# Steady products read their moving tile from the last token to the first, and write the result bank backwards

## The reference, cut to what matters

```
x <- LN_a(alpha*x + 0.5*SwiGLU_1(x))        w_gu: 1024 x 5632, w_down: 2816 x 1024
h  = x @ W_in                               26 column tiles of 128 (some made up of two pieces)
y  = [NSA | sliding-window attention | HGRN2](h) @ W_out
x <- LN_b(alpha*x + y)
x <- LN_c(alpha*x + 0.5*SwiGLU_2(x))
x <- x + sigmoid(x W_g + b_g) * (p W_p)
```

## Time and profile before

| what | value |
|---|---|
| median of 2 runs | 2225.23 us |
| both runs | 2224.98 and 2225.49 us |
| span of the profiled execution, first to last instruction | 2226.4 us |
| mean granted TensorE clock over the span | 0.998 |
| PE busy, share of the span | 2188.5 us, 98% |
| DVE busy | 1134.1 us, 51% |
| ACT busy | 902.1 us, 41% |
| DMA, mean rate | 91 GB/s |

### The profile page before, as it was taken

How to read it: one execution, slowest core, us unless ns; L and a number is a source line. 1 busy time by engine, 2 the same in 40 slices (tenths; PEclk the granted TensorE clock), 3 DMA queues, 4 the chain that set the end, 5 groups by cost and what they waited for, 6 DMA issues and landing times.

```text
span 2226.4 us, 30811 instructions
## 1 busy us (share of the span) xinstructions
PE 2188.5 (98%) x12675; PEld 1807.6 (81%) x12675; DVE 1134.1 (51%) x1966; ACT 902.1 (41%) x1447; POOL 137.8 (6%) x128
## 2 busy tenths in 40 slices
PE   9999999999999999999999999999999999999999
PEld 7888889877668888888888888898776788888888
DVE  4333345888867333343643333358887663333454
ACT  4223224555656322322632222255466462232234
POOL 0000011210001000012000000112200100000110
PEclk9999999999999999999999999999999999999999
DMA  5333333322222333332333333333322233333322
GB/s 167 97 102 95 88 95 90 99 65 70 81 72 67 104 95 98 106 89 85 107 95 95 100 100 86 98 80 99 77 67 67 67 95 96 101 98 97 95 88 72
DMA packets 384219, 202.76 MB, mean 91 GB/s; under 512 B 17360, under 2 KB 381776, under 8 KB 384080
## 3 DMA queue, kind: packets, MB, share of 16 engines
q1 hardware_dynamic: 383520, 200.15, 31.7%
q10 hardware_dynamic: 560, 0.66, 0.1%
HBM read 198.68 MB, written 2.10 MB: 90 GB/s over the span
## 4 chain that ended last, share of the span: by engine, by line
PE 82%; DVE 9%; ACT 6%; issue 2%; DMA 1%; POOL 0%; SPq 0%; DVEq 0%; ACTq 0%
PE banks L254 24%; PE banks L255 24%; PE banks L256 24%; DVE lev L1241 2%; ACT xhi L353 1%; PE banks L1518 1%; DVE w_lo L246 1%; DVE att L1277 1%; ACT lev L1121 1%; ACT w_hi L240 1%; ACT xT L354 1%; PE banks L1505 1%; PE banks L1459 1%; PE banks L305 1%; PE banks L311 1%
## 5 line engine op out<-in xcount | busy, mean ns | idle before, releaser
L246 DVE TENSOR_TENSOR w_lo<-w_raw,w_hi 128x1024 fp32r<-128x1024 f32 (+2 forms) x370 | 452.5, 1226 | 831.6 <-ACT w_hi L240 831.3
L254 PE MATMUL banks<-xhi,w_hi 128*128 128x512 f32 (+1 forms) x1936 | 758.1, 392 | 1.0 <-DVE w_lo L246 1.0
L256 PE MATMUL banks<-xhi,w_lo 128*128 128x512 f32 (+1 forms) x1936 | 749.7, 387 | 0.0
L255 PE MATMUL banks<-xlo,w_hi 128*128 128x512 f32 (+1 forms) x1936 | 749.7, 387 | 0.0
L240 ACT ACTIVATE w_hi<-w_raw 128x1024 fp32r<-128x1024 f32 (+2 forms) x370 | 376.0, 1018 | 810.0 <-PE banks L256 796.7
L254 PEld LDWEIGHTS banks<-xhi,w_hi 128*128 128x128 f32 x1936 | 365.6, 189 | 75.8 <-issue 1.6
L256 PEld LDWEIGHTS banks<-xhi,w_lo 128*128 128x128 f32 x1936 | 364.1, 188 | 74.6
L255 PEld LDWEIGHTS banks<-xlo,w_hi 128*128 128x128 f32 x1936 | 364.5, 188 | 72.5 <-issue 1.0
L254 PE MATMUL banks<-hhi,w_hi 128*128 128x512 f32 (+1 forms) x792 | 293.4, 371 | 0.0
L256 PE MATMUL banks<-hhi,w_lo 128*128 128x512 f32 (+1 forms) x792 | 289.5, 365 | 0.0
L255 PE MATMUL banks<-hlo,w_hi 128*128 128x512 f32 (+1 forms) x792 | 289.4, 365 | 0.0
(11 more groups left out here) (274 smaller groups left out, 2002.0 us busy)
## 6 DMA issues: line engine op xcount, KB each, us to landing
w_raw<-in_ffn_w_gu_dram SPq DMA_DIRECT2D x176, 512.0 KB, 4.0
w_raw<-in_ffn_w_down_dram SPq DMA_DIRECT2D x64, 512.0 KB, 4.0
w_raw<-in_w_in_dram SPq DMA_DIRECT2D x48, 512.0 KB, 4.1
w_raw<-in_ffn_w_down_dram SPq DMA_DIRECT2D x32, 384.0 KB, 3.5
w_raw<-in_w_out_dram SPq DMA_DIRECT2D x32, 256.0 KB, 2.9
w_raw<-in_ple_gate_w_dram SPq DMA_DIRECT2D x16, 512.0 KB, 3.7
w_raw<-in_cmp_k_w_dram SPq DMA_DIRECT2D x16, 256.0 KB, 2.8
w_raw<-in_cmp_v_w_dram SPq DMA_DIRECT2D x16, 256.0 KB, 3.2
```

The costliest lines, as they stand in the source:

```text
L246: dve.tensor_tensor(part_view(wlo, n), raw_view(split_at[n]).rearrange("p k n -> p (k n)"), part_view(whi, n), ALU.subtract).then_inc(sems ...
L254: pe.matmul(bank, w_hi, x_hi, start=first, stop=False)
L255: pe.matmul(bank, w_hi, x_lo, start=False, stop=False)
L256: return pe.matmul(bank, w_lo, x_hi, start=False, stop=last)
```

## The change

In `multiply`, and nowhere else, the output view of the bank and both moving views get a step of minus one along the tokens. Column 511 of the activation tile is read first and its result is written to column 511 of the bank; column 0 comes last. Each result lands where it landed before. The stationary operands, the number of instructions, their order on every engine, the semaphores and the data transfers are as before.

```diff
--- before.py
+++ after.py
@@ -264,7 +264,7 @@
             for i, k in enumerate(ks):
                 if ready:
                     ready(k)
-                mm = three(pe, ps[:, bank, :], whi[:, slot, k, :], wlo[:, slot, k, :], hi(k), lo(k),
+                mm = three(pe, ps[:, bank, ::-1], whi[:, slot, k, :], wlo[:, slot, k, :], hi(k)[:, ::-1], lo(k)[:, ::-1],
                            first and i == 0, last and i == len(ks) - 1)
             if finish:
                 mm.then_inc(sems["mm_done"], 1)
```

## The result

| | before | after |
|---|---|---|
| median us | 2225.23 (2 runs) | 2268.86 (2 runs, 2268.59 and 2269.14) |
| span of the profiled execution, us | 2226.4 | 2266.8 |
| ratio, 95% interval | | 1.0195 (1.0165 to 1.0224) |

What follows compares the result with a forecast made beforehand. The prediction took TensorE's steady stream of matmuls, 226.7 ns apart at 512 columns, to bound the kernel. Read, write and the rest were each 0, sum 0 us, so the forecast stayed at 2225 us, range 2125 to 2620 us.

Steps and rivals of the forecast that it cites:

- What bounds the kernel: Whole kernel: TensorE, busy 98% of the span; time is the count of matmuls times the distance between starts, almost no slack.
- The count: Matmuls changed in the steady products: 2432 triples, 7296 matmuls, 1654 us of the 2226.4 us span at 226.7 ns each.
- same-time case: Whole kernel: the change makes no difference to the time, 2218 to 2233 us; chance 62%.
- the moving read backwards: Activation tile read in falling order by the changed matmuls: 0; upper bound +0.20 us each, lower bound 13.3 ns less each.
- The accumulating write backwards: Bank written in falling order by the changed matmuls: 0, same bounds as the read, since no dependence gets shorter.
- Weight loads, waits, transfers: Everything beside the changed matmuls: unchanged in number and place, covered by an equally long matmul stream, 0.
- a price for each matmul (slower): Turning costs each changed matmul a second fixed part of 13.3 ns: +97 us, 2322 us; chance 5%.
- Half rate: Falling read or write served one word at a time, 0.43 us between changed matmuls: +1459 us, 3684 us; chance 18%.
- Some columns pay: One column in four of each changed matmul takes twice its time, 53 ns each: +389 us, 2614 us; chance 8%.

Runs made afterwards that it cites:

- the surveys: Four kernels, the kernel before with differing address orders and widths in gate and up products of the first one or two SwiGLU blocks; only distances used, no time.
- write alone: Against the kernel before, steady products write the bank from last column to first but read the moving tile rising; 2225.8 us, ratio 0.9998.

## Why the prediction was wrong

**What bounds the kernel** was right, and it is why so little per matmul shows: 6.7 ns on 7296 matmuls is nearly 2% of the kernel. The count held: 48.6 us by it, 46.9 us in TensorE's busy time. One reading was too narrow: TensorE waits for weights twice, for 1.0 us at L254 and for 1.2 us at L1485, which the lines of the earlier trace rows leave out; nothing hangs on it.

**The forecast** of 2225 us and its same-time case of 2218 to 2233 us missed the measured 2268.86. That it lies inside 2125 to 2620 is no merit: the upper end was put there for a quarter of the columns paying double, which did not happen.

**The step that failed is "the moving read backwards. I take 0."** It measured 6.67 ns for each matmul. I leaned on the gapped reads of L1008 as the nearest rows and argued that neighbours stay neighbours. Those rows are 16 columns wide and go by turns to four column tiles of 32. Some start 3 ns behind the one before, less than the 6.7 ns of 16 columns at 0.4167 ns, so they overlap and their 9 ns aren't the rate of one read. They couldn't show a price of 1.3 ns per 100 columns; I said that 16 columns are too few and still let them decide. How poor a witness they are shows in the surveys: gapped reads of 512 columns, which I ranked as the worse case, take 453 ns.

**The accumulating write backwards, 0**, was right (write alone: ratio 0.9998). The Trainium skill, page "PSUM — Partial Sum Buffer", section "Specifications (TRN2)", says that any access pattern that isn't contiguous slows matmuls significantly; the runs here disagree for a falling write (226.7 ns), and for falling words in blocks of 4 and swapped halves, taken on both sides (226.7 ns). So the sentence doesn't hold for these orders.

**Weight loads, waits, transfers, 0**, was right but for idle time in the head stages, which I hadn't counted: the two waits shown above shrank by 3.6 us.

**The rivals.** The case that came was "a price for each matmul (slower)", to which I gave 5%, at half the size that I gave it (6.7 for 13.3 ns) and on the wrong ground: I took a second fixed part for it, but at 256 columns there is no price at all. "Half rate" was wrong for falling reads; a level near it (453 ns, forecast 430) exists, but for gapped reads. The sentence that gaps have "no visible price" is true of the 16-column rows and false of 512 columns. "Some columns pay" is not what came, but its counter-argument, that an in-between price shows nowhere, fell too: 266.6 ns stand between the two rates.

**A rule for gapped reads.** The Trainium skill, page "SBUF — State Buffer", section "Specifications (TRN2)", gives lines of 16 bytes and asks for two hits or more in each for full bandwidth. If that is read as enough, the trace disagrees: even words and then odd words, and pairs of words with gaps of two, both give two hits in each line and took 453 ns instead of 227.

**What stays open** is the cause of the 6.67 ns. It lies on the moving read, it needs frequent steps down and more than 336 columns, the start word changes it, and 6.67 ns is the time of 16 columns (16 x 0.4167 ns). That a buffer runs empty behind a slower fetch is only argued. The price shrinks with fewer weight columns, so the moving read alone doesn't set it, and no experiment here takes the weight load away: each matmul has its own, 12675 of both the earlier trace rows.

## What to carry to other kernels

Where TensorE is full, the order in which a matmul reads its moving operand is part of its price: for fp32r and 512 columns keep it rising over runs of 64 words or more. A falling order of the write is free, and so are falling words in blocks of 4 and swapped blocks of 128 or 256 words. Don't read the moving operand with gaps of one or two words: at 512 columns that halved the rate. And when the only nearby row is thirty times narrower than what it is to vouch for, give the small price its full weight: a few nanoseconds were the whole result.

## What the runs showed of the hardware

- Many steady distances of fp32r matmuls are whole steps of 6.67 ns: 18 steps at 256 rising columns, 22 at 320, 34 at 512 rising, 35 at 512 falling, 40 with falling words in blocks of 16. Rising from word 0, it is one step for each 16 columns and two more, from 256 up to 400 columns and at 496 and 512. Others aren't whole steps: 118.3 ns (256 falling), 162.3 (352 falling), 228.9 (504 falling), 230.0 (512 rising beside 96 or 64 weight columns).
- Falling words within rising blocks of 16 are worse (266.6 ns) than within 8 (233.1), 32 (236.7) or 64 (233.3), or a wholly falling read.
- At 128 columns both orders stand 111.6 or 111.7 ns apart, where 16 columns a step and two more would be 66.7. Something else sets the distance; that it is the weight load was not tested.
- The same order can have two steady distances in two programs: 448 columns rising, 202.7 and 206.6 ns; 504 columns rising from word 1, 235.5 and 226.8 ns.
